# A two-layer pair of sequence models on one core: the normed operand placed at another byte distance from the split weights, one distance per stage

## The chip, the cores and the metric

The kernel runs on one core of a Trainium2 chip. The metric is the device time of that core in microseconds. Engines are named as in the profile: PE (matmul), PEld (loading the stationary operand of a matmul, beside PE), DVE, ACT, POOL, SP (which issues the DMAs).

## What is computed

Two models of two layers each, one behind the other, on 256 tokens of width 1024, all in float32. Before each block there is an RMS norm `u = norm(h) * g`, and most of the work is products of `u` with weights that are used once:

```python
def mixer_block(h, ...):                 # layers ("mix", 0), ("mix", 1)
    u = rmsnorm(h, g_norm)
    proj = u @ w_in                      # 1024 x 9280
    ...                                  # retention, gated delta rule, gates
    return h + merged @ w_out
# ffn 0: h + (silu(u @ wg) * (u @ wu)) @ wd, width 2816      stage ("ffn", 0)
# ffn 1: a mixture of 8 experts, top 2, width 1408           stage ("ffn", 1)
# behind each: h + sigmoid(rmsnorm(h) @ w_ple_gate) * (p @ w_ple)
# second model, two layers: u @ w_in_2 (1024 x 3656)         stages ("n1", 0), ("n1", 1)
#                           relu(u @ w_up_2)**2 @ w_down_2, width 4096   ("n2", 0), ("n2", 1)
```

## The kernel before

**Split operands.** Each float32 operand of a large product is held as two parts of type fp32r, high and low. `mm3` (L495) issues three matmuls for one product of 128 rows: weight high by operand high, weight high by operand low, weight low by operand high. These three are called a triple here. In the columns of the profile a matmul is written out<-moving,stationary, so a triple of a projection reads `ps<-uh,whi`, `ps<-ul,whi`, `ps<-uh,wlo`, each with 256 moving columns (the tokens) and 128 stationary columns of weights.

**The weights.** SP brings them in pieces of up to 1024 columns a partition into `raw`. ACT writes the high part into one of four slots of `whi`, DVE the low part into the same slot of `wlo`. A slot is 4096 bytes a partition. A stationary tile of 128 columns lies at a multiple of 512 bytes in its slot.

**The normed operand.** `self.U` (L302) is a pair, high part in the tensor `uh` and low part in `ul`, 2048 columns each (8 tiles of 256 tokens, k = 0 to 7), and all stages use this one pair but for the gate product behind each block, which has a pair of its own at the start of the arena. `OFF = 16` leaves 64 bytes free ahead of each part. The class `Tiles` (L184 to L199) puts tile k = 7 another `STEP = 8` columns (32 bytes) further on.

**Addresses.** Tensors are laid down one behind another in the order of `Memory.__init__`, each rounded up to 32 bytes: `whi` 16384 bytes a partition, `wlo` 16384, `h` 8192, `uh` 8320, `ul` 8320, then `ident_r`, `router_hi`, `router_lo`, `scr`, `rst`, `eps`, `flag` (19520 together) and the arena. "Distance" in what follows is the first byte of the moving tile less the first byte of the stationary tile, modulo 256. It is the same for every slot and every tile of weights: 64 for `uh` and 192 for `ul` (8320 is 128 more than a multiple of 256); for k = 7 it is 96 and 224; for every operand in the arena whose columns start at a multiple of 64 it is 64, the high and the low part alike. Such are the hidden units of the feed-forward stages (`M.hid`), the outputs of the mixers (`M.ret`, `M.gop`, `M.mp`, `M.mixp`) and the gate product's pair (`M.pleU`).

**Order of the work.** PE follows an order that is written out: in the mixers (`TENSOR_A`, `TENSOR_B`) single pieces of projections, 8 triples each, take turns with short float32 matmuls of the recurrences. In the feed-forward stages `hidden` issues all products of a group of hidden units with `u`, 8 triples (k = 0 to 7) a unit and matrix, and `down` then issues the products of these units with the second matrix. `values` uses `u` as the stationary operand and up to 512 columns of weights as the moving one. The experts read a gathered copy of `u` as the stationary operand; for every other pair of experts this copy (`UG[1]`) lies in `uh` and `ul`.

**Writers and readers of the pair.** Ahead of a stage ACT writes `uh` (`gain`, L1440), DVE writes `ul` (`low`, L2207); `opening` in both writes the scaled pair once more.

Of the kernel before, what the change touches and what calls it, by code (L numbers as in the profile page):

```python
# [10 lines left out]
F32R = mybir.dt.float32r  # L11
# [10 lines left out]
AHEAD = 3  # L22
OFF = 16
STEP = 8
ARENA = 23128
CAP = 128
ALL = slice(None)
# [108 lines left out]
def v3(ap, n=T):  # L136
    return ap.rearrange("p (a t) -> p a t", t=n)
# [152 lines left out]
class Memory:  # L290


    def __init__(self, nc, ctx, drams):
        def sb(name, n, dt=F32):
            return ctx.enter_context(nc.sbuf_tensor(name, [P, n], dt))[:, :]

        self.stream, self.small, self.const, self.xT, self.pT, self.blocks, self.out = drams
        self.SM, self.CO = sb("SM", small_layout()[1]), sb("CO", const_layout()[1])
        raw = sb("raw", NRAW * CH)
        self.whi, self.wlo = sb("whi", NSPLIT * CH, F32R), sb("wlo", NSPLIT * CH, F32R)  # L300
        self.h, uh, ul = sb("h", 2048), sb("uh", 2048 + 2 * OFF, F32R), sb("ul", 2048 + 2 * OFF, F32R)
        self.hT, self.U = v3(self.h), tuple(Tiles(x[:, OFF:2048 + 2 * OFF]) for x in (uh, ul))  # L302
        self.identr = sb("ident_r", P, F32R)
        self.router = [v3(sb(x, 64, F32R), 8) for x in ("router_hi", "router_lo")]
        self.scrs, self.rsts = sb("scr", 7 * 512), sb("rst", 2 * 512)
        self.eps, self.flag = sb("eps", 4), sb("flag", 1, I32)
        with nc.sbuf_tensor("arena", [P, ARENA], F32) as t:
            self.AR = t[:, :]
        self.ARr = sb("arena_r", ARENA, F32R)
        self.ps = ctx.enter_context(nc.psum_tensor("ps", [P, 8, 512], F32))  # L310
        self.scols, self.ccols = small_layout()[0], const_layout()[0]
        self.ident, self.onesrow = self.co("ident"), self.co("ones")
        self.ones = self.onesrow[:, 0:P]
        self.epsc = self.eps[:, 0:1]
        self.A, self.B = self.arena(SPEC_A), self.arena(SPEC_B)
        self.rsum = self.A["cols"][:, 64:72]
        self.r1, self.gains = self.B["r1"], self.B["gains"]
        self.pler = self.AR[:, 13312:13824]
        self.plep = (v3(self.ARr[:, 13824:14336]), v3(self.ARr[:, 14336:14848]))
        self.plet = v3(self.AR[:, 14848:14848 + 2048])  # L320
        self.pleU = (v3(self.ARr[:, 0:2048]), v3(self.ARr[:, 2048:4096]))
        self.mixp = (v3(self.B["mixh_r"]), v3(self.B["mix_r"]))

        self.late = self.B["hg"][:, 0:384]
        self.pa = [v3(self.B[x], 512) for x in ("pa", "hE")]
        self.hid = [tuple(v3(self.ARr[:, i * 5632 + j * 2816:i * 5632 + (j + 1) * 2816]) for j in range(2))
                    for i in range(2)]
        A = self.A
        self.at = [v3(A[x], P) for x in ("AT", "VN")]
        self.qkd = [v3(A[x], P) for x in ("QKD", "D")]  # L330
        self.kd, self.vn = [v3(A[x], P) for x in ("S", "X")], v3(A["AT"], P)
        self.block, self.inv = (v3(A["S"][:, i * 256:(i + 1) * 256], 16) for i in range(2))
        self.wide = [A[x][:, 512:1024] for x in ("S", "Y")]
        self.part = [A["Y"][:, i * 64:(i + 1) * 64] for i in range(2)]
        self.ret = (v3(A["gz_r"]), v3(A["rg_r"]))
        self.gop = (v3(A["qkv_r"][:, 0:2048]), v3(A["qkv_r"][:, 2048:4096]))
        at = sum(n for _, n in SPEC_A[:7])
        self.mp = (v3(self.ARr[:, at:at + 2048]), v3(self.ARr[:, at + 2048:at + 4096]))

        AR, ARr = self.AR, self.ARr  # L340
        self.g = AR[:, 17000:17600]
        self.iota, self.iocol = self.g[:, 456:584], self.g[:, 432:433]
        self.rows8 = [AR[0:8, 20672 + i * T:20672 + (i + 1) * T] for i in range(6)]
        self.rows8r = ARr[0:8, 20672 + 4 * T:20672 + 5 * T]
        self.uN = [ARr[:, i * 2048:(i + 1) * 2048].rearrange("p (t d) -> p t d", t=2) for i in range(2)]

        at = 4096 + OFF
        self.UG = [[Tiles(ARr[:, at + i * (2048 + 2 * OFF):at + (i + 1) * (2048 + 2 * OFF)]) for i in range(2)], self.U]
        at += 2 * (2048 + 2 * OFF)
        self.HT = [v3(ARr[:, at + i * 1408:at + (i + 1) * 1408], P) for i in range(2)]  # L350
        self.YP = [ARr[:, 17600 + i * 1024:18624 + i * 1024] for i in range(2)]
        self.SEL = v3(ARr[:, 19648:20160])
        self.SELT = [ARr[:, 20160 + z * T:20160 + (z + 1) * T] for z in range(2)]
        self.gs = [self.g[:, 440 + 2 * z:442 + 2 * z] for z in range(2)]
        at = const_layout()[0]["ret"][0]
        self.raw = [raw[:, i * CH:(i + 1) * CH] for i in range(NRAW)]
        self.raw += [self.CO[:, at + i * CH:at + (i + 1) * CH] for i in range(2)]
        self.raw += [AR[:, 11264 + i * CH:11264 + (i + 1) * CH] for i in range(3)]
        self.over = (AR[:, 13312:14336], ARr[:, 11264:12288], ARr[:, 12288:13312])
# [41 lines left out]
                        "n2": "norm2_g_2"}[tag[0]], tag[1])  # L401

    def operand(self, tag):
        return self.pleU if tag[0] == "ple" else self.U

    def factor(self, tag, slot):

# [72 lines left out]
class Tensor(Program):  # L480
# [487 lines left out]
    def moe(self, meanwhile):  # L968
# [5 lines left out]
        self.wait_ge(*K.when("router"))  # L974
        for k in range(8):
            self.wait_ge(*K.when(*self.u_ready(k)))
            last = self.mm3(b[0:8, 0:T], pick(M.router, ALL, k, ALL), pick(M.U, ALL, k, ALL), k == 0, k == 7)
        last.then_inc(*s("ps", "lgt"))
        self.sums(("ffn", 1), (3,))
        embed = meanwhile()  # L980
# [8 lines left out]
        for i in range(2):  # L989
            if i:  # L990
                self.columns(("ffn", 1))
            for t in range(2):
                for h in range(2):
                    b = self.bank(self.work, "un", i, t, h)
                    for k in range(4):
                        last = self.mm(b[:, k * P:(k + 1) * P], M.U[i][:, h * 4 + k, t * P:(t + 1) * P], M.identr, True, True)
                    last.then_inc(*s("ps", "un", i, t, h))
        b = self.bank(self.work, "gsel")
        self.wait_ge(*K.when("gates"))
# [374 lines left out]
class Scalar(Program):  # L1374
# [99 lines left out]

    def opening(self, tag, first, end):

        s, U = self.main, self.M.U
        for _ in range(4):
            self.ahead()
        self.factors(tag)  # L1480
        self.ahead()
        self.columns(tag)
        self.wait_ge(*self.K.when("rc", tag))
        first()
        for q in range(4):
            if q:
                self.ahead()
            x = self.M.scr(self.scr.take("nu", tag, q))
            self.wait_ge(*self.K.when("nu", tag, q))
            self.wait_ge(*self.K.when("u0 done", tag, q))  # L1490
            self.act(U[0][:, 2 * q:2 * q + 2, :], v3(x), ACT.Copy).then_inc(*s("u1h", tag, q))
        end()
# [665 lines left out]
class Vector(Program):  # L2158
# [56 lines left out]

    def opening(self, tag):

        K, M, s, U = self.K, self.M, self.main, self.M.U
        for _ in range(4):
            self.ahead()  # L2220
        if tag == DOUBLE:
            x = self.rst("rs", tag)
            self.wait_ge(*K.when("r1"))
            self.tt(x[:, T:2 * T], x[:, 0:T], self.bank("norm", tag)[:, T:2 * T], MUL).then_inc(
                *s(("v2",), ("free", "norm", tag)))
            self.wait_ge(*K.when("r2"))
            self.tt(x[:, T:2 * T], x[:, T:2 * T], M.r1, MUL).then_inc(*s("rs", tag))
        g, r = M.gain(tag), self.factor(tag)

        def scaled(q):  # L2230
            x = self.scr("nu", tag, q)
            self.wait_ge(*K.freed("nu", tag, q))
            for k in range(2):
                last = self.stt(x[:, k * T:(k + 1) * T], M.hT[:, 2 * q + k, :], g[:, 2 * q + k:2 * q + k + 1], r, MUL, MUL)
            last.then_inc(*s("nu", tag, q))

        def low(q):
            self.wait_ge(*K.when("u1h", tag, q))
            self.tt(U[1][:, 2 * q:2 * q + 2, :], v3(self.scr("nu", tag, q)), U[0][:, 2 * q:2 * q + 2, :].bitcast(F32),
                    SUB).then_inc(*s(("u1", tag, q), ("free", "nu", tag, q), *([("free", "rs", tag)] if q == 3 else [])))  # L2240
        self.ahead()
        self.wait_ge(*K.when("rs", tag))
        scaled(0)
        scaled(1)
        self.ahead()
        scaled(2)
        low(0)
        scaled(3)
        self.ahead()
        low(1)  # L2250
        self.ahead()
        low(2)
        low(3)
# [1162 lines left out]
```

## Times and profile before

| | |
|---|---|
| two runs | 2138.79 and 2142.22 us |
| median | 2140.51 us |
| span of the profiled execution | 2140.0 us |
| PE busy | 2083.7 us, 97% of the span |
| PEld busy | 1944.3 us, 91% |
| DVE, ACT | 1531.2 us (72%), 1361.4 us (64%) |
| matmul records | 15388, of them 3 x 2240 with `uh` or `ul` as the moving operand |

Matmuls are pipelined: the duration of one (280 ns) overlaps those of its neighbours. What a matmul costs the engine in a dense run is the time from its start to the start of the next, and that is read from the starts in the timeline or from the length of a stretch divided by the matmuls in it.

### The profile page before, as it was taken

The numbers are of one execution on the slowest core, as the hardware profiler recorded it, in microseconds if no ns is written. First come the engines' busy times: TensorE is split into PE (matmuls) and PEld (weight loads), VectorE is DVE, ScalarE is ACT, GpSimd is POOL, SyncE is SP. The second block draws the span as 40 slices with busy tenths as digits, with TensorE's granted clock in tenths as the row PEclk, the third lists the DMA queues.
The fourth block names the chain that finished last, engine by engine and source line by source line (L and its number), as shares of the span: only waits on it lengthen the run. The fifth ranks groups of instructions, "written<-read, shape, count | busy, mean of one in ns | idle before, by whom it ended". The sixth has DMA issues, their size and how long they took to land.

```text
span 2140.0 us, 37171 instructions
## 1 busy us (share of the span) xinstructions
PE 2083.7 (97%) x15388; PEld 1944.3 (91%) x15388; DVE 1531.2 (72%) x2200; ACT 1361.4 (64%) x1879; POOL 65.4 (3%) x102
## 2 busy tenths in 40 slices
PE   8999999999999989999999999999999999999999
PEld 7988999999989889998888888888889999979999
DVE  6777556766577675566999899977868665876664
ACT  5765575554567755657777777776766545776553
POOL 0013000000000130000000000000000000000000
PEclk9999999999999999999999999999999999999999
DMA  7424345565554343455999999954415565524554
GB/s 272 149 95 139 99 155 175 180 193 188 169 172 153 96 142 98 150 183 189 337 331 334 334 333 333 349 192 151 131 60 179 189 194 163 158 70 138 190 191 133
DMA packets 126448, 400.59 MB, mean 187 GB/s; under 512 B 26048, under 2 KB 26432, under 8 KB 126272
## 3 DMA queue, kind: packets, MB, share of 16 engines
q1 hardware_dynamic: 126272, 398.14, 56.0%
q8 instruction: 123, 2.02, 0.4%
q14 instruction: 53, 0.43, 0.1%
HBM read 395.72 MB, written 2.36 MB: 186 GB/s over the span
## 4 chain that ended last, share of the span: by engine, by line
PE 81%; ACT 8%; DVE 7%; issue 2%; POOL 2%; DMA 1%; SPq 0%; ACTq 0%; DVEq 0%; POOLq 0%
PE ps L493 80%; DVE wlo L2186 2%; ACT whi L1409 2%; ACT arena L1419 2%; ACT scr L1419 2%; DVE arena L2194 1%; ACT L1419 1%; DVE arena L2186 1%; POOL arena L3166 1%; ACT L1413 1%; DVE scr L2186 1%; POOL arena L3169 1%; DVE h L2186 1%; ACT rst L1419 1%; PE ps L1086 0%
## 5 line engine op out<-in xcount | busy, mean ns | idle before, releaser
L2186 DVE TENSOR_TENSOR wlo<-raw,whi 128x1024 fp32r<-128x1024 f32 (+2 forms) x622 | 745.5, 1212 | 283.7 <-ACT whi L1409 278.5
L1409 ACT ACTIVATE whi<-raw 128x1024 fp32r<-128x1024 f32 (+2 forms) x622 | 643.1, 1042 | 321.9 <-PE ps L493 315.2
L493 PE MATMUL ps<-uh,whi 128*128 128x256 f32 x2240 | 644.2, 288 | 10.9 <-DVE arena L2194 4.2
L493 PE MATMUL ps<-uh,wlo 128*128 128x256 f32 x2240 | 632.2, 282 | 0.0
L493 PE MATMUL ps<-ul,whi 128*128 128x256 f32 x2240 | 625.8, 279 | 0.0
L493 PE MATMUL ps<-arena_r,whi 128*128 128x256 f32 x2720 | 473.4, 279 | 2.9 <-DVE arena_r L2186 2.0
L493 PEld LDWEIGHTS ps<-uh,whi 128*128 128x128 f32 x2240 | 420.2, 188 | 23.9 <-issue 14.6
L493 PEld LDWEIGHTS ps<-ul,whi 128*128 128x128 f32 x2240 | 421.8, 188 | 4.2 <-issue 3.8
L493 PEld LDWEIGHTS ps<-uh,wlo 128*128 128x128 f32 x2240 | 419.4, 187 | 0.0
L493 PEld LDWEIGHTS ps<-arena_r,whi 128*128 128x128 f32 x2720 | 411.6, 188 | 5.8 <-DVE arena_r L2186 3.4
L493 PE MATMUL ps<-arena_r,wlo 128*128 128x256 f32 x1360 | 376.7, 277 | 0.0
L493 PEld LDWEIGHTS ps<-arena_r,wlo 128*128 128x128 f32 x1360 | 255.3, 188 | 0.0
L493 PE MATMUL ps<-whi,arena_r 128*128 128x512 f32 (+1 forms) x736 | 228.8, 387 | 0.0
L493 PE MATMUL ps<-arena 128*128 128x128 f32 (+3 forms) x1360 | 158.7, 290 | 11.9 <-DVE arena L2186 6.9
L493 PEld LDWEIGHTS ps<-arena 128*128 128x128 f32 (+2 forms) x1360 | 144.3, 190 | 24.1 <-issue 12.5
L493 PEld LDWEIGHTS ps<-whi,arena_r 128*128 128x128 f32 x736 | 137.7, 188 | 26.4 <-DVE wlo L2186 0.3
L493 PE MATMUL ps<-wlo,arena_r 128*128 128x512 f32 (+1 forms) x368 | 141.5, 385 | 0.0
L493 PE MATMUL ps<-whi,uh 128*128 128x512 f32 (+2 forms) x352 | 131.0, 372 | 10.5 <-DVE wlo L2186 9.6
L493 PE MATMUL ps<-whi,ul 128*128 128x512 f32 (+2 forms) x352 | 128.7, 366 | 0.0
L493 PE MATMUL ps<-wlo,uh 128*128 128x512 f32 (+2 forms) x352 | 128.1, 364 | 0.0
L1419 ACT ACTIVATE arena<-ps 128x512 f32<-128x512 f32 (+5 forms) x125 | 65.2, 536 | 93.1 <-PE ps L493 83.2
L2186 DVE TENSOR_TENSOR wlo<-arena,whi 128x1024 fp32r<-128x1024 f32 (+1 forms) x84 | 95.5, 1158 | 11.6 <-ACT whi L1409 10.8
(186 smaller groups left out, 2186.8 us busy)
## 6 DMA issues: line engine op xcount, KB each, us to landing
raw<-stream SPq DMA_DIRECT2D x586, 512.0 KB, 4.2
arena<-stream SPq DMA_DIRECT2D x64, 512.0 KB, 5.6
CO<-stream SPq DMA_DIRECT2D x44, 512.0 KB, 5.4
raw<-stream SPq DMA_DIRECT2D x32, 384.0 KB, 4.4
arena<-stream SPq DMA_DIRECT2D x20, 384.0 KB, 4.3
CO<-stream SPq DMA_DIRECT2D x12, 384.0 KB, 4.6
CO<-const SPq DMA_DIRECT2D x3, 683.0 KB, 6.9
h<-xT SPq DMA_DIRECT2D x4, 256.0 KB, 6.4
```

What stands on the lines that cost most here:

```text
L493: return self.e.matmul(o, l, r, start=start, stop=stop, skip_group_check=True)
L1409: self.e.activation(M.whi[:, b:b + n], M.raw[a][:, 0:n], ACT.Copy).then_inc(K.sem("weight_hi"), 1)
L1413: self.e.preload_act_table_set("natural_log_exp_and_others")
L1419: return self.e.activation(o, a, f, bias=bias, scale=scale, accum_out=acc)
L2186: return self.e.tensor_tensor(o, a, b, op)
L2194: return self.e.scalar_tensor_tensor(out=o, in0=a, scalar=x, in1=b, op0=op0, op1=op1)
L3166: self.e.tensor_tensor(x, block[:, j, j + 1:16].unsqueeze(2).broadcast_to([P, n, w]), inv[:, j, 0:w].unsqueeze(1).broadcast_to([P, n, w]), ...
L3169: self.e.tensor_tensor(inv[:, j + 1:16, 0:w], inv[:, j + 1:16, 0:w], x, ADD).then_inc(*s())
```

## The change

The two tensors `uh` and `ul` become one, `u`, of 4416 columns. For each stage a pair of views is made in it: the high part starts `at` columns into the tensor, the low part 2304 columns (9216 bytes, a multiple of 256) behind the high one, and both are dense, with no step before tile 7. `at` is the entry of the stage in `PLACE`.

| stage | at | distance, both parts | triples with 256 moving columns |
|---|---|---|---|
| mix 0 | 44 | 176 | 520 |
| ffn 0 | 52 | 208 | 352 |
| mix 1 | 16 | 64 | 520 |
| ffn 1 (router) | 16 | 64 | 8 |
| n1 0 | 40 | 160 | 168 |
| n2 0 | 49 | 196 | 256 |
| n1 1 | 56 | 224 | 168 |
| n2 1 | 20 | 80 | 256 |

The experts' copy keeps its bytes (`OFF`, 2080 columns apart, with the step at tile 7). All tensors behind `u` lie 1024 bytes further on.

```diff
@@ -22,6 +22,9 @@
 OFF = 16
 STEP = 8
+NORMED = 2208
+PLACE = {("mix", 0): 44, ("ffn", 0): 52, ("mix", 1): 16, ("ffn", 1): 16, ("n1", 0): 40, ("n2", 0): 49, ("n1", 1): 56,
+         ("n2", 1): 20}
@@ -298,8 +301,9 @@
-        self.h, uh, ul = sb("h", 2048), sb("uh", 2048 + 2 * OFF, F32R), sb("ul", 2048 + 2 * OFF, F32R)
-        self.hT, self.U = v3(self.h), tuple(Tiles(x[:, OFF:2048 + 2 * OFF]) for x in (uh, ul))
+        self.h, u = sb("h", 2048), sb("u", 2 * NORMED, F32R)
+        self.hT = v3(self.h)
+        self.U = {tag: tuple(v3(u[:, i * 2304 + at:i * 2304 + at + 2048]) for i in range(2)) for tag, at in PLACE.items()}
@@ -345,7 +349,8 @@
-        self.UG = [[Tiles(ARr[:, at + i * (2048 + 2 * OFF):at + (i + 1) * (2048 + 2 * OFF)]) for i in range(2)], self.U]
+        self.UG = [[Tiles(ARr[:, at + i * (2048 + 2 * OFF):at + (i + 1) * (2048 + 2 * OFF)]) for i in range(2)],
+                   [Tiles(u[:, OFF + i * (2048 + 2 * OFF):(i + 1) * (2048 + 2 * OFF)]) for i in range(2)]]
@@ -401,7 +406,7 @@
     def operand(self, tag):
-        return self.pleU if tag[0] == "ple" else self.U
+        return self.pleU if tag[0] == "ple" else self.U[tag]
...
@@ -1474,7 +1479,7 @@
     def opening(self, tag, first, end):
-        s, U = self.main, self.M.U
+        s, U = self.main, self.M.operand(tag)
```

The places that named `M.U` (router and transposition in `moe`, `opening` of ACT and DVE) now name the stage's own pair. No instruction is added or taken away.

## Rows read from the trace of the kernel before

**Rows 1.** The page: span, engines, PE clock in 40 slices, the chain by engine and line

```profile
span 2140.0 us, 37171 instructions
...
PE 2083.7 (97%) x15388; PEld 1944.3 (91%) x15388; DVE 1531.2 (72%) x2200; ACT 1361.4 (64%) x1879; POOL 65.4 (3%) x102
...
PEclk9999999999999999999999999999999999999999
...
PE 81%; ACT 8%; DVE 7%; issue 2%; POOL 2%; DMA 1%; SPq 0%; ACTq 0%; DVEq 0%; POOLq 0%
```

**Rows 2.** The page's groups: count | busy us, mean ns | idle before

```profile
L493 PE MATMUL ps<-uh,whi 128*128 128x256 f32 x2240 | 644.2, 288 | 10.9 <-DVE arena L2194 4.2
...
L493 PE MATMUL ps<-whi,uh 128*128 128x512 f32 (+2 forms) x352 | 131.0, 372 | 10.5 <-DVE wlo L2186 9.6
```

**Rows 3.** Windows, PE alone: from:to us, length, PE busy (matmuls), clock, DMA share, GB/s

```profile
36.00:383.00 347.00, 337.24 (x2729) 0.99 0.45 140
...
453.38:515.71 62.33, 62.33 (x531) 1.00 0.63 192
515.71:575.50 59.79, 59.79 (x530) 1.00 0.62 195
...
1819.00:1932.00 113.00, 107.04 (x810) 0.97 0.34 108
```

**Rows 4.** Groups by form of the two middle windows of rows 3, PE

```profile
L493 PE MATMUL ps<-uh,wlo 128*128 128x256 f32 x176 | 49.7, 282 | 0.0
...
L493 PE MATMUL ps<-arena_r,wlo 128*128 128x256 f32 x176 | 48.6, 276 | 0.0
```

**Rows 5.** Timeline of PE, end of `hidden`, start of `down`: start us, length, what

```profile
512.88 0.28 PE L493 MATMUL ps<-uh,whi 128*128 128x256 f32 x1
...
515.35 0.28 PE L493 MATMUL ps<-uh,whi 128*128 128x256 f32 x1
515.47 0.28 PE L493 MATMUL ps<-ul,whi 128*128 128x256 f32 x1
515.59 0.28 PE L493 MATMUL ps<-uh,wlo 128*128 128x256 f32 x1
515.71 0.39 PE L493 MATMUL ps<-arena_r,whi 128*128 128x256 f32 x2
...
516.05 0.39 PE L493 MATMUL ps<-arena_r,whi 128*128 128x256 f32 x2
```

**Rows 6.** Timeline of PE, the gate product behind ffn 0

```profile
575.56 3.02 PE L493 MATMUL ps<-scr,CO 128*128 128x256 f32 x12
...
578.78 0.40 PE L493 MATMUL ps<-arena_r,whi 128*128 128x256 f32 x2
...
583.02 0.40 PE L493 MATMUL ps<-arena_r,whi 128*128 128x256 f32 x2
...
583.37 1.03 PE L493 MATMUL ps<-scr,CO 128*128 128x256 f32 x4
...
584.58 0.39 PE L493 MATMUL ps<-arena_r,whi 128*128 128x256 f32 x2
...
600.90 0.39 PE L493 MATMUL ps<-arena_r,whi 128*128 128x256 f32 x2
```

**Rows 7.** Timeline of PE, `values` with 512 moving columns, opening of mix 0

```profile
29.17 0.39 PE L493 MATMUL ps<-whi,uh 128*128 128x512 f32 x1
...
33.34 0.39 PE L493 MATMUL ps<-whi,uh 128*128 128x512 f32 x1
```

**Rows 8.** Waits of PE over the span, the longest: total us, times, longest us

```profile
PE ps L493 <- DVE wlo L2186: 12.2, 7, 9.6
PE ps L493 <- DVE arena L2186: 6.9, 4, 1.9
```

**Rows 9.** The writers of the pair, by tile `uh`: ns min/median/max, first to last start

```profile
L1419 ACT ACTIVATE uh<-h,SM x56: 492/495/514, 6.4 to 1959.2; 128x256 fp32r<-128x256 f32 x56
L2194 DVE SCALAR_TENSOR_TENSOR ul<-h,SM,uh x56: 471/479/1520, 7.0 to 1959.7; 128x256 fp32r<-128x256 f32 x56
```

More of the change, by code:

```diff
@@ L976, in moe @@
             self.wait_ge(*K.when(*self.u_ready(k)))
-            last = self.mm3(b[0:8, 0:T], pick(M.router, ALL, k, ALL), pick(M.U, ALL, k, ALL), k == 0, k == 7)
+            last = self.mm3(b[0:8, 0:T], pick(M.router, ALL, k, ALL), pick(self.U, ALL, k, ALL), k == 0, k == 7)
         last.then_inc(*s("ps", "lgt"))
@@ L995, in moe @@
                     for k in range(4):
-                        last = self.mm(b[:, k * P:(k + 1) * P], M.U[i][:, h * 4 + k, t * P:(t + 1) * P], M.identr, True, True)
+                        last = self.mm(b[:, k * P:(k + 1) * P], self.U[i][:, h * 4 + k, t * P:(t + 1) * P], M.identr, True, True)
                     last.then_inc(*s("ps", "un", i, t, h))
@@ L2216, in opening @@
     def opening(self, tag):
-        K, M, s, U = self.K, self.M, self.main, self.M.U
+        K, M, s, U = self.K, self.M, self.main, self.M.operand(tag)
         for _ in range(4):
```

## The prediction

> **What bounds the kernel.** I read the page first: PE is busy for 2083.7 of 2140.0 us at full granted clock (2.4 GHz, all slices at 9 or more tenths), and four fifths of the chain are PE [rows 1]. PE waits for others seldom; the largest single cause over the whole span is 12.2 us [rows 8]. So the time is a count of matmuls times what each costs from start to start, and an edit counts as far as it changes that cost. The groups say where: 2240 triples have the normed operand as the moving one, 352 more have it as the stationary one [rows 2].
>
> Next come windows laid over dense runs, in which PE has no idle time. In ffn 0 the 176 triples of the second `hidden` take 62.33 us, 354.1 ns a triple or 118.0 ns a matmul. The 176 triples of the `down` behind it take 59.79 us, 339.7 ns a triple or 113.2 ns a matmul [rows 3, 4]. Same engine, shapes, clock and weight slots; 4% apart. Different are the operand (64/192 against 64/64, in the sense of distance given above) and the order in which PSUM is written.
>
> The timeline takes the 354.1 apart. From k = 0 to k = 7 a unit takes 515.35 - 512.88 = 2.47 us for 7 triples, 352.9 ns each; the triple of k = 7, at 96/224, takes 0.36 us; the first triple of `down` 0.34 [rows 5]. Rounded starts allow 353 and 359 or 360, and 7 x 353.4 + 359.5 over 8 is the 354.1 of the window.
>
> The gate product is the row on which most hangs. It has one operand pair, at 64/64 throughout. Behind the float32 sums it runs from 578.78 to 583.02, 12 triples in 4.24 us or 353.3 ns each; behind the next sums from 584.58 to 600.90, 48 triples in 16.32 us or 340.0 ns [rows 6]. So at 64/64 there are two courses, a slow one of 353.3 and a quick one of 340.0, and what went just before chooses; once in a course a dense run stays there. I infer that the load of the next stationary tile and the stream of the moving one get in each other's way in the slow course and miss each other in the quick one. The trace doesn't show the collision itself. In `hidden`, at 64/192, the quick course does not appear even though a run can last 176 triples.
>
> **The change, part by part.** *Instructions.* None comes or goes, so no wait, DMA or queue position changes. The writers of the pair take about 0.5 us a tile of 256 columns whatever its start: 56 of ACT at 495 ns, 56 of DVE at 479 ns [rows 9]. I cost their new starts at 0. If a start that isn't a multiple of 32 bytes cost them a tenth, the eight tiles ahead of a stage would be ready 8 x 0.05 = 0.4 us later, hidden in part by the first products, under 3 us over eight stages.
>
> *The arena* moves by 1024 bytes, a multiple of 256. Each product there keeps its distances; I cost it at 0. The experts' copy keeps its bytes: 0.
>
> *The step at tile 7 goes.* In a slow run that saves 359.5 - 353.4 = 6 ns in 8 triples, 0.8 ns a triple; over 2240 it is 1.8 us, the smallest gain if nothing else alters. But the step did another thing: `down` behind it comes in at 340 from its second triple on [rows 5], while a 64/64 run behind float32 work may start in the slow course [rows 6]. There are 688 such `down` triples (176 + 256 + 256). Should all fall into the slow course, that costs 688 x 13.3 = 9.2 us. Now the kick comes from the change of distance between stages instead (208, 196 or 80 to 64). I take one tenth of it, 0.9 us.
>
> *Both parts at one distance.* The trace has no row at 176, 208, 160, 196 or 80 for both. The nearest rows bound a triple: 340.0 from below (quick course, no start-to-start time in a dense run is under 113 ns), and from above three matmuls like the high ones of the 96/224 triple. 359.5 with 116 for its low one, as the middle start shows within 10 ns, leaves 121.7, three of them 365. From 354.1 that is 14.1 gained or 10.9 lost a triple, over all 2240 a gain of 31.6 us or a loss of 24.4 us. I lean to the quick side. The one alike pair that the trace has takes the quick course in `down` and most of the gate product; the one unlike pair never does. And where the run is long, one passage into the quick course pays for the rest of it.
>
> The stages: ffn 0 and both n2 have 864 triples in long runs with little float32 work between. Three quarters in the quick course give 864 x 14.1 x 0.75 = 9.1 us. Mix 0 and both n1 have 856, in pieces of 8 to 80 that start anew behind float32 matmuls; half quick gives 856 x 14.1 x 0.5 = 6.0 us. Their slow remainders (216 + 428) save the step: 0.5 us. Mix 1 and the router stay at 64 and begin behind float32 work; I leave them slow, 528 x 0.8 = 0.4 us. In the mixers PE has some 10 us idle in 347 [rows 3], so little of the gain can turn into waiting there; I take off 0.5 us. `values` has 160 triples of its own outside the experts. At 512 columns 6 triples take 4.17 us, 695 ns each [rows 7], against twice the quick 340, so 15 ns a triple is at stake; 160 of them make 2.4 us at most, either way, and I take 0.
>
> Sum: 9.1 + 6.0 + 0.5 + 0.4 - 0.5 - 0.9 = 14.6 us. Against the profiled execution: 2140.0 - 14.6 = 2125.4; the median of the runs is 0.5 us above the span, and I give 2125 us.
>
> A rule of the Trainium skill speaks against all of it. Its page "SBUF — State Buffer", section "Who interferes with whom", gives PE two independent read ports, one for the moving operand and one for the weight load, and has only the port pair shared by DVE and GpSimd contend. By that rule distance can't matter and the time stays at 2140; that 12 triples took 353.3 and 48 triples 340.0 at one and the same distance [rows 6] does not fit PE's two reads being independent, but does not prove that distance governs them either.
>
> **Rivals.**
>
> *Nothing but the step (chance 0.27).* What chooses the course is what precedes a run, not the distance. All stages with the pair alike start behind float32 work and stay at 353.3, like the first 12 triples of the gate product. Gain 1.8 us, 2138. For it: [rows 6], same addresses, both courses. Against it: 64/192 never enters the quick one. A full absence of any effect of place would end at 2140, 2 us from it.
>
> *Collisions at the new distances (chance 0.18), slower.* 80 lies beside 96, 160 to 224 beside 192 and 224, and the triple at 96/224 is the slowest. If the stages with a new distance, 1720 triples, run at 359.5, that is 1720 x 5.4 = 9.3 us lost; with all `down` runs thrown into the slow course 9.2 more; mix 1 gives 0.4 back: 2158. It decides from a mean of 355 ns a triple at these distances once the `down` runs are lost. Worst by the bound of 365: 18.7 + 9.2 = 28, 2168. For it: the step was there for a purpose, as the entry to `down` shows. Against it: only 96 is known to be bad, 224 was the cheap matmul of that triple.
>
> *Quick everywhere (chance 0.05 within 2%).* 31.6 us gained, 2108.
>
> *Below the quick course (chance 0.05), faster by over 2%.* 113.3 ns is 272 periods of 2.4 GHz for 256 columns. If the 16 over are also a matter of place, 2240 x (354.1 - 320) = 76 us, 2064. No dense row under 113 speaks for it.
>
> **Numbers.** Forecast 0.45, around 2125, own range 2112 to 2134. Low end 2108, all quick; high end 2152, where the collisions come in half of their stages; beyond it lie the full slower rival and, below, the last one, together under 2 in 10. Two per cent, 43 us, is about what a measurement of this kernel tells from no change; the loss bound of 28 us doesn't reach it and the gain bound of 32 us neither. So within 2%: 0.93; faster 0.05; slower 0.02.
>
> **What would show each step.** PE's matmul count unchanged. The same stretch of ffn 0, 176 triples: 60 us if quick, 62.2 if slow, 63 or more if colliding. `down` behind it 59.8, or 62.2 if it lost its kick. In the timeline steady triples at 340.0 or 353.3 with no slower eighth one. n2 stages of 64 triples: 21.8 quick against 22.6. Mix 1 as before. The forecast is wrong if these stretches stay at 353 a triple, if a third value appears, or if `down` changes course.

## The result, and the profile after

| | before | after |
|---|---|---|
| median of the runs | 2140.51 us | 2162.61 us (two runs, 2162.51 and 2162.70) |
| ratio | | 1.0096, interval 1.0074 to 1.0119 |
| span of the profiled execution | 2140.0 us | 2160.7 us |
| PE busy | 2083.7 us | 2107.7 us |

The changed kernel is 1% slower: 22 us lost where 15 had been forecast as gained, and 10 us above the upper end of the range (2152). The page of after, beside [rows 1]: the same count of matmuls, PE 24.0 us busier, DVE and ACT as before. The clock line has the same digits, but the mean granted clock over the span is 0.992 against 0.995 before; that comes up again below.

```profile
span 2160.7 us, 37171 instructions
...
PE 2107.7 (98%) x15388; PEld 1968.5 (91%) x15388; DVE 1532.6 (71%) x2200; ACT 1361.9 (63%) x1879; POOL 65.3 (3%) x102
...
PEclk9999999999999999999999999999999999999999
...
PE 82%; ACT 7%; DVE 6%; POOL 2%; issue 2%; DMA 0%; SPq 0%; ACTq 0%; DVEq 0%; POOLq 0%
```

PE's waits of after, beside [rows 8]: 12.2 and 6.9 have become 11.8 and 6.9. No new wait has come in.

```profile
PE ps L498 <- DVE wlo L2191: 11.8, 8, 9.1
PE ps L498 <- DVE arena L2191: 6.9, 4, 1.9
```

So the loss lies in what a matmul costs. "Quick" below is the course at 340 ns a triple, "slow" the one at 353, and a triple is called steady if it took under 380 ns, so that pauses are left out. Windows of after, PE alone, columns as in [rows 3], from three answers: mix 0; the second `hidden` of ffn 0 and the `down` behind it (176 triples each); then the same pair for a group of n2 0 and a `hidden` of n2 1 (64 triples each).

```profile
36.00:386.00 350.00, 340.15 (x2722) 0.99 0.44 139
...
457.25:520.17 62.92, 62.92 (x530) 1.00 0.58 191
520.17:582.36 62.19, 62.19 (x530) 1.00 0.58 188
...
1739.73:1763.10 23.37, 23.37 (x195) 1.00 0.61 182
1763.10:1785.73 22.63, 22.63 (x195) 1.00 0.58 185
...
2088.90:2111.94 23.04, 23.04 (x195) 1.00 0.53 182
```

Divide by the triples. `hidden` of ffn 0 at distance 208: 62.92 / 176 = 357.5 ns, before 354.1. `hidden` of n2 0 at 196: 23.37 / 64 = 365.2. `hidden` of n2 1 at 80: 23.04 / 64 = 360.0. And `down`, whose operand and weights keep their distance: 62.19 / 176 = 353.4, before 340.1; in n2 0 22.63 / 64 = 353.6. (The window in [rows 3] ends 0.06 us too early, at 575.50; the next matmul starts at 575.56 [rows 6], so `down` took 59.85 us before, not 59.79.) The timeline of after where `down` begins, beside [rows 5]:

```profile
520.05 0.28 PE L498 MATMUL ps<-u,wlo 128*128 128x256 f32 x1
520.17 0.40 PE L498 MATMUL ps<-arena_r,whi 128*128 128x256 f32 x2
...
520.53 0.40 PE L498 MATMUL ps<-arena_r,whi 128*128 128x256 f32 x2
...
520.88 0.40 PE L498 MATMUL ps<-arena_r,whi 128*128 128x256 f32 x2
```

Starts 0.36 and 0.35 us apart: the slow course from the first triple on, where before the second one was at 340.

I summed, from start to start, every triple with 256 moving columns in both traces, stage by stage (us):

| triples | before | after | |
|---|---|---|---|
| normed operand, mix 0 (distance 176) | 195.3 | 195.4 | steady triples 353.8 to 357.8 ns; see the clock below |
| ffn 0 (208) | 125.8 | 127.0 | |
| mix 1 (64) | 192.7 | 193.8 | 34 of 520 quick; see the clock below |
| n1 0 (160), n1 1 (224) | 128.8 | 128.7 | |
| n2 0 (196), n2 1 (80) | 183.3 | 187.2 | |
| arena: `down` and gate product of ffn 0, PLE products | 87.6 | 90.9 | 239 of 256 quick before, none after |
| arena: `down` of n2 0 and n2 1 | 173.8 | 180.6 | 508 of 511 quick before, none after |
| arena: outputs of the mixers, gate product behind ffn 1 | 215.5 | 216.5 | 201 quick before, 116 after |

The arena's part is 11.1 us, the normed operand's 6.2. The remaining 3.4 us of the 20.7 between the spans go with the clock. Windows of before, then of after (the columns of [rows 3], the fifth is the granted clock):

```profile
182.56:185.97 3.41, 3.41 (x18) 0.50 0.02 5
```

```profile
144.03:154.26 10.23, 10.23 (x46) 0.50 0.02 3
...
782.32:785.73 3.41, 3.41 (x19) 0.50 0.02 5
```

A clock of 0.50 is the lower level, 1.2 GHz. Before has six such stretches of 3.4 us, 20.5 us in all; after has seven and one of 10.2 us, 34.1 in all. Most of their matmuls are the short ones between the triples. The order of the matmuls is the same in both traces, so they can be laid side by side: those between the triples cost 5.9 us more where either trace is at 1.2 GHz, and 1.9 us less elsewhere. The first of the two lines from after shows the largest piece; the 44 matmuls that start in it took 7.1 us before and take 10.2. The groups of the two pages:

```profile
L493 PE MATMUL ps<-arena 128*128 128x128 f32 (+3 forms) x1360 | 158.7, 290 | 11.9 <-DVE arena L2186 6.9
```

```profile
L498 PE MATMUL ps<-arena 128*128 128x128 f32 (+3 forms) x1360 | 163.7, 296 | 10.5 <-DVE arena L2191 6.9
```

The clock also explains two odd rows of the table. One stretch at 1.2 GHz fell on triples of mix 0 in before and of mix 1 in after. That hides 1.6 us of what distance 176 cost mix 0, and it is why mix 1 took 1.1 us more although its steady triples were slightly cheaper. Such stretches come and go between runs of one and the same kernel: beside the later experiments the kernel before took 2135.2 us at a mean clock of 0.997 and 2150.8 us at 0.989. So these 3 to 4 us can't be put down to the change, and single spans are compared below only together with the windows. At 1.2 GHz a triple took the same 640 ns in both, from start to start:

```profile
183.47 0.41 PE L493 MATMUL ps<-uh,whi 128*128 128x256 f32 x1
...
184.11 0.41 PE L493 MATMUL ps<-uh,whi 128*128 128x256 f32 x1
```

```profile
783.13 0.63 PE L498 MATMUL ps<-u,whi 128*128 128x256 f32 x2
...
783.77 0.63 PE L498 MATMUL ps<-u,whi 128*128 128x256 f32 x2
```

### The profile page after: what moved, and what is told of

Read it like the earlier page. It is cut to its first block, busy times and chain, and to the rows that moved or that the text cites. A ratio compares the mean times of both kernels' runs of the same rounds, so it can differ in the third digit from the quotient of the medians.

```text
span 2160.7 us, 37171 instructions
## 1 busy us (share of the span) xinstructions
PE 2107.7 (98%) x15388; PEld 1968.5 (91%) x15388; DVE 1532.6 (71%) x2200; ACT 1361.9 (63%) x1879; POOL 65.3 (3%) x102
## 4 chain that ended last, share of the span: by engine, by line
PE 82%; ACT 7%; DVE 6%; POOL 2%; issue 2%; DMA 0%; SPq 0%; ACTq 0%; DVEq 0%; POOLq 0%
PE ps L498 81%; DVE wlo L2191 2%; ACT scr L1424 2%; ACT arena L1424 2%; ACT whi L1414 2%; DVE arena L2199 1%; DVE arena L2191 1%; ACT L1424 1%; POOL arena L3171 1%; ACT L1418 1%; POOL arena L3174 1%; DVE h L2191 1%; DVE scr L2191 1%; ACT rst L1424 0%; PE ps L1091 0%
## 5 line engine op out<-in xcount | busy, mean ns | idle before, releaser
L498 PE MATMUL ps<-u,whi 128*128 128x256 f32 (+1 forms) x4480 | 818.9, 285 | 10.4 <-DVE arena L2199 3.9
L498 PEld LDWEIGHTS ps<-u,whi 128*128 128x128 f32 (+1 forms) x4480 | 690.2, 188 | 27.5 <-issue 17.7
L498 PE MATMUL ps<-u,wlo 128*128 128x256 f32 x2240 | 630.7, 282 | 0.0
L498 PE MATMUL ps<-arena_r,whi 128*128 128x256 f32 x2720 | 484.5, 281 | 2.8 <-DVE arena_r L2191 1.9
L498 PEld LDWEIGHTS ps<-u,wlo 128*128 128x128 f32 x2240 | 421.4, 188 | 0.0
L498 PE MATMUL ps<-whi,u 128*128 128x512 f32 (+2 forms) x704 | 203.9, 369 | 9.9 <-DVE wlo L2191 9.1
L498 PEld LDWEIGHTS ps<-whi,u 128*128 128x128 f32 x704 | 128.5, 190 | 29.8 <-DVE wlo L2191 9.1
L498 PE MATMUL ps<-wlo,u 128*128 128x512 f32 (+2 forms) x352 | 128.4, 365 | 0.0
L2191 DVE TENSOR_TENSOR wlo<-arena,whi 128x1024 fp32r<-128x1024 f32 (+1 forms) x84 | 95.5, 1158 | 11.6 <-ACT whi L1414 10.8
L1414 ACT ACTIVATE whi<-arena 128x1024 fp32r<-128x1024 f32 (+1 forms) x84 | 84.8, 1011 | 26.6 <-PE ps L498 26.3
L1424 ACT ACTIVATE scr<-ps 128x256 f32<-128x256 f32 (+1 forms) x94 | 42.3, 450 | 85.3 <-PE ps L498 85.2
```

The lines of the kernel that those rows point to most:

```text
L498: return self.e.matmul(o, l, r, start=start, stop=stop, skip_group_check=True)
L1414: self.e.activation(M.whi[:, b:b + n], M.raw[a][:, 0:n], ACT.Copy).then_inc(K.sem("weight_hi"), 1)
L1424: return self.e.activation(o, a, f, bias=bias, scale=scale, accum_out=acc)
L2191: return self.e.tensor_tensor(o, a, b, op)
```

## The experiments

A distance is that of both parts unless two are given. The runs of the kernel before beside them had medians of 2140.55 to 2142.96 us.

### All stages at 64, dense

```diff
+PLACE = {("mix", 0): 16, ("ffn", 0): 16, ("mix", 1): 16, ("ffn", 1): 16, ("n1", 0): 16, ("n2", 0): 16, ("n1", 1): 16, ("n2", 1): 16}
```

> The changed kernel with the distance 64 in all eight stages, both parts alike and dense. Theory of the step (the 32-byte step at tile 7 is what puts the stage behind it into the quick course, 340 ns a triple instead of 353.3): without it all 688 down triples stay slow, the operand's own triples run at 353.3; 2140 - 1.8 + about 11 = 2149 us. Theory of the distance alone (what was lost was lost at the new distances): down is quick again, 2138 us.

Measured: 2146.56 us, ratio 1.0008 (0.9988 to 1.0028). Windows of ffn 0, `hidden` and `down`:

```profile
456.23:518.42 62.19, 62.19 (x530) 1.00 0.63 193
518.42:580.61 62.19, 62.19 (x531) 1.00 0.61 188
```

Both parts alike isn't enough for the quick course: 353.4 ns in both. Of 2097 steady triples 225 were quick, mostly in the short projections of the second model. `down` was slow here as well, in every triple, though its own distance is that of before. The run times alone don't tell this kernel from the one before (the interval holds 1); the reading rests on the trace, in which the arena's triples take 10.6 us more and the normed operand's 1.0 less.

### The kernel before without its step

```diff
-        self.hT, self.U = v3(self.h), tuple(Tiles(x[:, OFF:2048 + 2 * OFF]) for x in (uh, ul))
+        self.hT, self.U = v3(self.h), tuple(v3(x[:, OFF:OFF + 2048]) for x in (uh, ul))
...
```

The experts' copy keeps its step, and the arena its address.

> The kernel before without the step at tile 7 of the normed operand (the experts' copy keeps it); parts still unlike, 64 and 192. Theory of the step: down falls into the slow course, 353.3 a triple, and the time is about 2149 us. Rival, the passage from unlike parts to alike ones is enough to reach the quick course: down stays at 340, 2138 us.

Measured: 2152.51 us, ratio 1.0054 (1.0031 to 1.0077), profiled span 2151.5.

```profile
452.58:514.77 62.19, 62.19 (x531) 1.00 0.63 193
514.77:576.96 62.19, 62.19 (x531) 1.00 0.60 188
```

`hidden` gains 0.14 us, the price of the dear triple; `down` loses 2.34 us against the 59.85 of before. Taking away the step alone costs 10.7 us in the medians and 11.5 us in the profiled spans. This is the first half of the loss, isolated, with every other address untouched: the step's work was to bring `down` in quick.

### The step put back in three ways

All at 64 with the step of 32 bytes (tile 7 at 96 for both parts; `PLACE` has 16 in every stage):

```diff
-        self.U = {tag: tuple(v3(u[:, i * 2304 + at:i * 2304 + at + 2048]) for i in range(2)) for tag, at in PLACE.items()}
+        self.U = {tag: tuple(Tiles(u[:, i * 2240 + at:i * 2240 + at + 2048 + 2 * STEP]) for i in range(2)) for tag, at in PLACE.items()}
```

> The changed kernel with distance 64 in all stages, both parts alike, and the 32-byte step at tile 7 back (tile 7 at 96, both parts). Theory of the step: down is quick, at most 2140 us; if the operand's own triples at 64/64 can be quick too once a step has passed, most of them run at 340 and the time falls to about 2115 us. Rival, only the unlike pair 96/224 leads into the quick course: down at 353, 2149 us or more.

Measured: 2153.99 us, ratio 1.0053 (1.0027 to 1.0079).

The changed kernel's distances with the same step (the diff above, `PLACE` as in after):

> The changed kernel with its own distances and the 32-byte step at tile 7 back. Theory that a step of 32 bytes as such is the kick: down at 340 behind ffn 0 and both n2, about 11 us less than 2162, so 2151 us. Rival, the place 96 (or 96/224) ahead of 64 is what counts, not the step: down stays at 353, 2160 to 2164 us.

Measured: 2158.67 us, ratio 1.0084 (1.0055 to 1.0113).

All at 64, but tile 7 at 96 and 224 as in the kernel before, from a list of starts per tile (an entry of `PLACE` is the start of the high part, of the low part, the odd tile, and its two starts; the same for all stages):

```diff
+PLACE = {("mix", 0): (16, 16, 7, 24, 56),
...
+        self.U = {tag: tuple(Spots(u, spots(i, *at)) for i in range(2)) for tag, at in PLACE.items()}
```

> Both parts at 64 in all stages, but tile 7 at 96 for the high part and 224 for the low one, as in the kernel before. Theory: the triple at 96/224 ahead of one at 64/64 is what leads from the slow course (353.3 ns a triple) to the quick one (340.0), which then holds for as long as the distances stay 64/64. So down is quick (340) as before, and from the second unit on the operand's own triples should be quick too, about 343 on the mean of eight with the odd one; in long runs (864 triples of ffn 0 and n2) that is 9.6 us less than before, in the mixers' long pieces some more: 2125 to 2131 us. Rival, 96/224 taken in the quick course leads back to the slow one: own triples alternate or stay at 353, down quick only by luck, 2140 to 2150 us.

Measured: 2153.77 us, ratio 1.0053 (1.0036 to 1.0070). The `down` windows of the three in this order, of the last one its `hidden` too:

```profile
516.38:578.57 62.19, 62.19 (x530) 1.00 0.61 188
```

```profile
517.14:579.33 62.19, 62.19 (x531) 1.00 0.60 189
```

```profile
457.18:519.50 62.32, 62.32 (x530) 1.00 0.62 191
519.50:581.70 62.20, 62.20 (x531) 1.00 0.60 189
```

None brings `down` of ffn 0 in. With the changed distances and the step one run of n2 0 (63 quick triples) came in quick, the other six runs of `down` did not. In ffn 0 the triple at 96/224 does nothing out of triples at 64/64; out of triples at 64/192, as in the kernel before, it does. A step is no remedy in itself. (The last kernel's profiled execution was the slowest of its five, 2161.49 us, at a mean clock of 0.989; its windows lie at full clock.)

The odd triple moved to tile 0 of each unit (against the run before):

```diff
-PLACE = {("mix", 0): (16, 16, 7, 24, 56),
+PLACE = {("mix", 0): (16, 16, 0, 24, 56),
...
```

> The same with the odd tile at k = 0 instead of 7, so that each piece of 8 triples begins with it. Theory: 359 + 344 + 6 x 340 = 2743 ns a piece of 8 against 2833 before, 11 ns a triple, in the short pieces of the mixers as well; down comes in from tile 7 at 64/64 in the quick course and stays. 2240 x 11 = 25 us less where PE sets the time: 2116 to 2124 us. Rival as for tile 7: one passage through 96/224 toggles the course, every other piece slow, 2135 to 2150 us.

Measured: 2152.52 us, ratio 1.0062 (1.0041 to 1.0082). `hidden` 62.34, `down` 62.18 us. It also ended quick runs: at the odd triple a run at 340 went 349, 350, 353 and stayed at 353.

### Which part of the odd triple counts

Steady triples at 64/64 (mix 1: 64/192), tile 7 at another pair in each stage: ffn 0 64/224, n2 0 96/64, n2 1 64/192, n1 0 96/192, n1 1 224/224, mix 0 224/96, mix 1 96/224.

> Both parts at 64 and an odd tile 7, of another kind in each stage, high/low: ffn 0 64/224, n2 0 96/64, n2 1 64/192, n1 0 96/192, n1 1 224/224, mix 0 224/96, mix 1 96/224 with the low part elsewhere at 192 (as before). It tells which half of 96/224 leads into the quick course, by the down stages behind ffn 0 and both n2. If the high part at 96 does it: down quick behind n2 0 alone. If the low part at 224 does it: quick behind ffn 0 alone. If any unlike triple does it: quick behind all three. If both halves are needed: all slow.

Measured in one run: 2153.2 us. Behind 64/224, 96/64 and 64/192 every `down` was slow, which by the expectation meant that both halves are needed. In mix 1, the one stage that repeats the kernel before, two runs of the mixer's output began at 344 and went on at 340, as in before: there the odd triple works. But `hidden` of ffn 0 was partly quick, 61.39 us, and its units of 8 triples show a strict cycle of three. Windows of four units in a row, then of the last unit and the first 8 triples of `down`:

```profile
463.78:466.51 2.73, 2.73 (x27) 1.00 0.67 189
466.51:469.33 2.82, 2.82 (x26) 1.00 0.31 99
469.33:472.16 2.83, 2.83 (x27) 1.00 0.81 249
472.16:474.89 2.73, 2.73 (x27) 1.00 0.41 131
...
514.06:516.79 2.73, 2.73 (x27) 1.00 0.80 299
516.79:519.62 2.83, 2.83 (x27) 1.00 0.32 75
```

A unit of 2.73 us has its first seven triples at 340. The 64/224 triple at its end throws the next unit into the slow course, the one after that leaves it there, and the third brings it back. So the low part at 224 alone does lead in, one time in three. `down` came behind a quick unit and was slow; the PLE product in the middle of ffn 0 came behind the second slow unit, was at 340 from its first triple on and handed the quick course to the unit behind it, at the same distance. What an odd triple does hangs on the course that it meets.

### The curve of distances

Each stage another distance: mix 0 0, ffn 0 128, mix 1 96, n1 0 32, n2 0 48, n1 1 112, n2 1 144.

> The changed kernel, dense and both parts alike, with distances that were not tried yet: mix 0 at 0, ffn 0 at 128, mix 1 at 96, n1 0 at 32, n2 0 at 48, n1 1 at 112, n2 1 at 144. It measures the cost of a triple by distance. Theory of the distance (what a triple costs is set by it): different steady values, between 340 and 369 ns as in the changed kernel, 96 near 365; down at 353 everywhere. Theory that distance plays no part: 353 everywhere.

Measured in one run: 2156.46 us. `hidden` of ffn 0 at 128 took 62.66 us, 356.0 ns a triple:

```profile
452.59:515.25 62.66, 62.66 (x531) 1.00 0.62 191
```

Then around 112, 4 bytes from stage to stage: mix 0 104, ffn 0 108, mix 1 112, n1 0 116, n2 0 120, n1 1 124, n2 1 100.

> The changed kernel with distances around 112: mix 0 at 104, ffn 0 at 108, mix 1 at 112, n1 0 at 116, n2 0 at 120, n1 1 at 124, n2 1 at 100. How wide the good place is: if it is a matter of 16-byte lines, 104 to 108 and 116 to 124 cost more than 112 or share a value within a line; if it is a wide basin, all lie near 340; if 112 was the stage, mix 1 is at 353.

Measured in one run: 2161.0 us. `hidden` of ffn 0 at 108 took 63.35 us, 359.9 a triple:

```profile
456.16:519.51 63.35, 63.35 (x530) 1.00 0.62 190
```

The mean of the steady triples of a stage (those under 380 ns), from these two traces and that of after:

| distance | ns a triple | distance | ns a triple |
|---|---|---|---|
| 0 | 359.3 | **112** | **342.5** (median 340.0) |
| 32 | 350.4 | 116 | 365.0 |
| 48 | 355.1 | 120 | 362.6 |
| 64 | 353.3 or 340.0 | 124 | 357.8 |
| 80 | 358.7 | 128 | 356.0 |
| 96 | 359.8 | 144 | 353.0 |
| 100 | 361.7 | 160 | 353.3 |
| 104 | 360.4 | 176, 208 | 357.8, 357.5 |
| 108 | 359.9 | 196, 224 | 365.0, 354.6 |

One distance stands out. At 112 all dense runs of four triples and more go to 340 within five triples, also behind float32 work, where 64 mostly stays at 353. Four bytes to either side it is gone. None of the new distances of the change is near it. Each distance stands for one stage here, but where one was had in two, the stage made no difference: 342.5 at 112 in n1 1 and in mix 1, each with its pieces of a few triples. `down`, at 64 in all of this, was slow but for one run of 64 triples behind distance 100.

At 1.2 GHz the differences are gone: in the traces of all these runs, whole triples well inside such stretches took 640 ns, at 0, 32, 64, 112 and 176 alike.

### All at 112

```diff
+PLACE = {("mix", 0): 28, ("ffn", 0): 28, ("mix", 1): 28, ("ffn", 1): 28, ("n1", 0): 28, ("n2", 0): 28, ("n1", 1): 28, ("n2", 1): 28}
```

> The changed kernel with distance 112 in all eight stages, the arena at 64 as before. Theory as for the weights moved: the normed operand's 2240 triples near 342. Down behind them at 64 holds the course in which it starts: 340 if the passage from 112 to 64 leaves the course alone (2112 to 2118 us in all), 353 if it does not (2121 to 2128 us). Rival, the stage and not the distance: 353 everywhere, 2145 to 2150 us.

Measured: 2130.14 us, ratio 0.9939 (0.9921 to 0.9957), faster than both kernels. Windows of ffn 0:

```profile
447.36:507.20 59.84, 59.84 (x531) 1.00 0.65 199
507.20:569.38 62.18, 62.18 (x530) 1.00 0.60 190
```

`hidden` is at 340.0 a triple now, `down` still at 353.3: its 64/64 has both courses, and a quick run at another distance just before it doesn't carry it in. Of the 100 dense runs of four and more triples of the normed operand 98 were quick within five triples, and none fell back into the slow course. The order in which PSUM is written, which the prediction had named as a second difference between `hidden` and `down`, is ruled out as the cause: it is the same here.

The same distance of 112 made by moving the weights by 208 bytes instead, for the operands in the arena too (`PLACE` has 16 in every stage):

```diff
-        self.whi, self.wlo = sb("whi", NSPLIT * CH, F32R), sb("wlo", NSPLIT * CH, F32R)
+        self.whi, self.wlo = (sb(x, NSPLIT * CH + 64, F32R)[:, 52:] for x in ("whi", "wlo"))
```

> The split weights lie 208 bytes further in their own tensors, the normed operand dense and both parts alike at its old place, so that every product with split weights, down and the mixers' outputs too, has the distance 112. In the run that measured distances, 150 triples at 112 came down to 340 ns within one to three triples after any start, in all other distances they did not. Theory that 112 draws a run into the quick course wherever it starts: all 3600 triples near 340, against before about 31 us less in the normed operand's and 5 us less in the arena's: 2103 to 2110 us. Rival, what was drawn in was the stage n1 1 and not the distance, or the place of both operands in their 64 bytes counts too: triples at 353, 2145 to 2150 us.

Measured: 2163.30 us, ratio 1.0095 (1.0059 to 1.0131).

```profile
455.35:518.71 63.36, 63.36 (x531) 1.00 0.61 188
518.71:582.07 63.36, 63.36 (x531) 1.00 0.61 185
```

360.0 ns in both. So either the distance isn't what counts, or weights that start at 48 modulo 64 spoil it (they start at 32 otherwise, by the sizes of the tensors ahead, if the first of these starts at a multiple of 64). The next runs tell which.

### Weights and operand moved together by 32 bytes

```diff
+        self.whi, self.wlo = (sb(x, NSPLIT * CH + 64, F32R)[:, 8:] for x in ("whi", "wlo"))
+PLACE = {("mix", 0): 36, ("ffn", 0): 36, ("mix", 1): 36, ("ffn", 1): 36, ("n1", 0): 36, ("n2", 0): 36, ("n1", 1): 36, ("n2", 1): 36}
```

> Weights moved by 32 bytes (start 64 modulo 256 instead of 32), U moved by as much, so that U stays at distance 112 while its own address is 176 instead of 144 modulo 256; the arena keeps its address and so comes to distance 32. Theory (the distance alone counts as long as the weights start at a multiple of 32): U stays at 340 to 342, and the operands of the arena take 350.4, the price of distance 32, instead of 353.3: `down` of ffn 0, 176 triples, 61.7 us; total 2128 to 2131. Rival (the operand's own address counts, not the distance to the weights): U takes the 353 of the place 144, 13 us more, and `down` stays at 353.3 or 340: 2140 to 2145. Second rival (the weights want their old address; with weights moved by 208 bytes everything took 360 although the distance was 112): U and the arena at 358 to 360, 2160.

Measured: 2131.96 us, ratio 0.9958 (0.9944 to 0.9973).

```profile
448.39:508.29 59.90, 59.90 (x531) 1.00 0.65 198
508.29:569.89 61.60, 61.60 (x531) 1.00 0.62 192
```

The normed operand stays at 340.3 at a new address of its own; `down`, whose operand did not move while its weights did, goes to 61.60 / 176 = 350.0, the price that distance 32 had in the curve. Between these two the distance decides, not the operand's address. With weights moved by 208 bytes something else comes on top. That it is their start off a multiple of 32 fits both runs, but only one such start was tried.

### The arena at 112 as well

The normed operand at 112, the weights where they were, and the whole arena, its float32 view too, 48 bytes further on:

```diff
-        self.ARr = sb("arena_r", ARENA, F32R)
+        self.ARr = sb("arena_r", ARENA + 12, F32R)[:, 12:]
...
```

> Normed operand at 112 in all stages, as in the run that was fastest so far (2130.1 us, where a triple of U took 340 to 342 and the 688 triples of `down` took 353.4 at 64/64), and the whole arena moved by 48 bytes, so that `down`, the gate product and the mixers' outputs lie at 112 too; the weights stay where they are. The parts of U now lie 8448 bytes apart instead of 9216, both multiples of 256. Theory (the distance decides the course, and an operand may start at any multiple of 16 bytes while the weights may not): `down` takes 340 a triple, 176 triples of ffn 0 in 59.9 us instead of 62.2, together with gate product and mixer outputs 11 to 13 us less than 2130.1, so 2117 to 2120. Rival A (the shared 48 bytes also touch what else lives in the arena, as the moved weights did): the gain is given back in other work, 2125 or more. Rival B (112 was good only for this tensor's own address, not as a distance): `down` at 353 to 360 as with the moved weights, 2130 to 2138.

Measured: 2117.41 us, ratio 0.9892 (0.9867 to 0.9917), 24 us less than the kernel before. Windows of ffn 0:

```profile
446.02:505.86 59.84, 59.84 (x530) 1.00 0.67 199
505.86:565.70 59.84, 59.84 (x530) 1.00 0.63 196
```

The page's line of the engines:

```profile
PE 2058.6 (97%) x15388; PEld 1919.0 (91%) x15388; DVE 1531.4 (72%) x2200; ACT 1361.7 (64%) x1879; POOL 65.2 (3%) x102
```

All 511 `down` triples of n2 are quick. PE is busy 25.1 us less than in [rows 1] and the span, 2115.8 us, is 24.2 us shorter: almost nothing is given back as waiting. The low part of the normed operand lies 8448 bytes behind the high one here, 9216 in the run with all at 112 before; only the second is a multiple of 512. The sum of its triples is 806.4 us in both, so counting the distance modulo 256 loses nothing here.

The changed kernel, distances kept, with only the arena moved:

> The changed kernel with its eight distances kept, and only the arena moved by 48 bytes to distance 112. It takes the dearer triples of U as they are and gives back what `down`, gate product and mixer outputs lost. Theory (of the 22 us that the change cost, some 11 are the lost quick course of the arena's operands): `down` at 340 whatever stage and distance went before, total 2162.6 - 11 to 13 = 2149 to 2152. Rival (the distance of U just before throws the run behind it into a slow course at 112 as well): `down` at 353 behind 196 and 80, total 2157 or more.

Measured: 2147.31 us, ratio 1.0029 (1.0011 to 1.0048).

```profile
451.99:514.90 62.91, 62.91 (x530) 1.00 0.63 192
514.90:574.79 59.89, 59.89 (x531) 1.00 0.63 193
```

`hidden` costs what it costs in after, `down` is quick behind 208, 196 and 80 alike (behind 208 its first triples take 349, 355, 357, then 340). That gives back 2162.6 - 2147.3 = 15.3 us, of which the arena's triples show 13.4. From there to the kernel with all at 112, 2147.3 - 2117.4 = 29.9 us, is the price of the change's distances against 112; the triples show 28.1 of it.

## Why the prediction was wrong

**The bound was right.** The time stayed within 2%, to which 0.93 had been given. PE bounds the kernel, every microsecond of a dense triple counts, waits stay as they are, `values` moved by nothing (its matmuls with `whi` take 369 ns on average, before 372 with `uh` and 366 with `ul`), and no writer of the pair came on the path. All of this was as the prediction had it. The split into two courses was right too, and so was the price of a fully lost `down`. "At full granted clock" was not quite so: the digits of the page hide six stretches at 1.2 GHz, and no term of the sum allowed for more or fewer of them.

**The step's term was sized at a tenth.** The prediction saw that the step might be what brings `down` in, worked out 9.2 us for losing it, and took 0.9, since the change of distance between stages would do instead. It did in none of the 688 triples. In the four traces with other distances (after, the same with the step, the two of the curve) there are 28 runs of `down`, and two of them came in quick, with 63 of 64 triples each: n2 0 behind 196 with the step, n2 1 behind 100. The kernel before without its step lost 10.7 us by this alone; the sums of the arena's triples grow by 10.8 there, 9.1 of it in `down`, the rest in the gate and PLE products and the mixers' outputs. [rows 5] had shown the entry; no row had shown any other entry that worked from a steady run of the normed operand. Nine tenths of a loss were written off on a mechanism without a row. And with 9.2 the term still leaves out the other products of the arena, 2.0 us in after.

**The lean to the quick side had no row for its distances.** The terms of 9.1 and 6.0 us assumed that both parts alike, at any distance, reach 340. They came out as 357.8 (176), 357.5 (208), 353.3 (160), 365.0 (196), 354.6 (224) and 358.7 (80), with not one quick triple at any of them. Over the 1720 triples of the stages with a new distance the mean is 358.2, against 353.9 before: 4.3 ns each, 7 us of steady cost (5 of them show in the sums above, since in mix 0 a stretch at 1.2 GHz fell away), where 15.1 were to be gained. What was taken for a property of "alike" was one of a single distance, 64, and even there of a minority: with all stages at 64 a tenth of the triples were quick. The bounds held, 340.0 below and 365 above; that the upper one was hit exactly, at 196, is luck, since it had been drawn from the triple at 96/224.

**Mix 1** was left slow and was nearly so: its steady triples took 352.4 ns against 352.9 expected.

**The arena** was costed at 0 since its distances are kept. They are, but at 64 the cost isn't given by the operand's own distance; it hangs on what ran before.

**The rival that came true** is that of collisions at the new distances with the `down` runs lost: 359.5 a triple assumed, 358.2 measured, 2158 against 2162.6. The arena's other products make 2 us of what it lacked (11.1 against 9.1 for `down`), the clock 3 to 4; the steady cost of the new distances was 7 where it had 9.3. It had a chance of 0.18, and the range stopped at half of it. The doubt that the prediction wrote beside it, "the step was there for a purpose", was the evidence that should have moved the chances: the trace showed the step's work, and showed nothing that would do it in its place.

The Trainium skill, page "SBUF — State Buffer", section "Who interferes with whom", has PE's two reads independent of each other. By that rule, the prediction said, distance can't matter and the time stays at 2140. Distance does matter: with the same instructions, the same weights and the same clock, `hidden` of ffn 0 takes 340.0 ns a triple at 112 and 359.9 at 108. Whether it is the two reads that get in each other's way no run shows.

What stays open: why 112, why the slow course at 64 is stable, and why the differences are gone at 1.2 GHz. The overlap of a weight load with the moving stream is a guess that no run tests.

## What to carry to other kernels

Where matmuls run densely and PE is the bound, treat the byte distance between the moving and the stationary operand as a parameter and measure it in one run that gives each stage another value. Take the value to which runs fall by themselves from any start, and bring every operand of the large products to it, the intermediate ones too; here that was worth 24 us of 2141. Where two courses exist, one window doesn't tell a matmul's price; look for the other course in the same trace. Before removing an irregularity in a tuned layout, look in the timeline at what follows it: the work that it helps may belong to another stage.

## What the hardware showed

- At 2.4 GHz three fp32r matmuls of 256 moving columns took 340 to 365 ns from start to start, with the distance as what was altered (7%), and 4 bytes matter: 359.9 at 108, 340.0 at 112, 365.0 at 116.
- At 1.2 GHz three of them took 640 ns at each of the distances 0, 32, 64, 112 and 176 that fell into such a stretch. That is one column a period of 1.2 GHz; 340 ns at 2.4 GHz is 16 periods more than the 256 columns for each matmul.
- At one distance there can be two stable courses: at 64 353.3 or 340.0 ns, each held through a run of 176 triples. At 112 runs come into the quick one by themselves, 98 of 100 within five triples.
- Moving weights and operand together by 32 bytes left 340.3; moving the weights alone by 208 bytes to the same distance gave 360.0. So the distance isn't all: where the weights start counts too.
- No dense triple with 256 columns was under 339 ns in any run.
